# The last attention by groups of four heads, its gate turned through memory ahead of the product

## The reference

```python
def swa_sinks(q, k, v, sinks):                    # after rms_norm and rope of q and k
    ...                                            # n = 2 blocks of 128; kk, vv: the block before and the own one
    scores = jnp.einsum('bnihgd,bnjhd->bnhgij', qb, kk).astype(jnp.float32) * (d ** -0.5)
    ...                                            # band: at most 127 tokens back
    m = jnp.maximum(jnp.max(scores, axis=-1, keepdims=True), sink)
    p = jnp.exp(scores - m)
    p = p / (jnp.sum(p, axis=-1, keepdims=True) + jnp.exp(sink - m))
    o = jnp.einsum('bnhgij,bnjhd->bnihgd', p.astype(v.dtype), vv)

def odd_mixer(h, w_in, q_norm_w, k_norm_w, sinks, w_out, pos):
    ...
    o = swa_sinks(q, k, v, sinks).reshape(b, s, ATTN_WIDTH)
    return (o * jax.nn.silu(gate)) @ w_out
```

## Time and profile before

| | |
|---|---|
| median of 3 runs (lowest, highest) | 1905.14 us (1904.91, 1905.21) |
| span of the profiled execution, from first to last instruction | 1903.2 us |
| PE busy | 1896.5 us, 100% |
| DVE busy | 1269.8 us, 67% |
| ACT busy | 1001.4 us, 53% |
| DMA | 375.85 MB, 197 GB/s over the span |

### The profile page before, as it was taken

One profiled execution on the slowest core, in us unless ns is written; L12 is line 12 of the kernel. 1 busy time (PEld: TensorE's weight loads), 2 busy tenths in 40 slices (PEclk: granted clock), 3 DMA queues, 4 the chain that ended last, 5 costly groups with the idle time before them and its releaser, 6 DMA issues.

```text
span 1903.2 us, 22788 instructions
## 1 busy us (share of the span) xinstructions
PE 1896.5 (100%) x8663; PEld 1561.5 (82%) x8663; DVE 1269.8 (67%) x1925; ACT 1001.4 (53%) x1410; POOL 14.4 (1%) x32
## 2 busy tenths in 40 slices
PE   9999999999999999999999999999999999999999
PEld 7888887888888888888888888888888888787887
DVE  6676566776666466665466776755766677777875
ACT  6777554454444344443444455654555554665653
POOL 0001000000000000000000000000000000000000
PEclk9999999999999999999999999999999999999999
DMA  9667754686666666666666686665676687555555
GB/s 326 199 189 183 208 178 133 200 258 195 194 192 196 192 188 193 197 195 195 192 194 193 219 268 194 194 192 175 196 210 194 192 261 214 164 170 165 153 170 177
DMA packets 212364, 375.85 MB, mean 197 GB/s; under 512 B 14672, under 2 KB 35968, under 8 KB 212256
## 3 DMA queue, kind: packets, MB, share of 16 engines
q1 hardware_dynamic: 211008, 371.65, 63.9%
q0 software_dynamic: 816, 2.11, 0.9%
q10 hardware_dynamic: 432, 0.66, 0.1%
HBM read 361.76 MB, written 12.60 MB: 197 GB/s over the span
## 4 chain that ended last, share of the span: by engine, by line
PE 98%; DVE 1%; ACT 0%; issue 0%; DVEq 0%; ACTq 0%
PE g L1151 31%; PE g L1153 31%; PE g L1152 31%; PE m L1220 1%; PE ob L1238 0%; PE ob L1237 0%; PE ob L1236 0%; PE m L1085 0%; DVE wl L1587 0%; PE m L1212 0%; PE m L1210 0%; PE m L1304 0%; PE ob L1291 0%; DVE st L1596 0%; PE ob L1285 0%; PE m L1093 0%
## 5 line engine op out<-in xcount | busy, mean ns | idle before, releaser
L1587 DVE TENSOR_TENSOR wl<-raw,wh 128x1024 fp32r<-128x1024 f32 (+1 forms) x660 | 802.6, 1217 | 555.3 <-ACT wh L1334 551.9
L1334 ACT ACTIVATE wh<-raw 128x1024 fp32r<-128x1024 f32 (+1 forms) x661 | 695.5, 1053 | 746.1 <-PE g L1153 739.4
L1151 PE MATMUL g<-wh,xh 128*128 128x512 f32 x1886 | 741.0, 393 | 0.0
L1153 PE MATMUL g<-wh,xl 128*128 128x512 f32 x1886 | 734.6, 389 | 0.0
L1152 PE MATMUL g<-wl,xh 128*128 128x512 f32 x1886 | 734.0, 389 | 0.0
L1151 PEld LDWEIGHTS g<-wh,xh 128*128 128x128 f32 x1886 | 354.1, 188 | 77.7 <-issue 4.8
L1153 PEld LDWEIGHTS g<-wh,xl 128*128 128x128 f32 x1886 | 354.0, 188 | 74.3
L1152 PEld LDWEIGHTS g<-wl,xh 128*128 128x128 f32 x1886 | 354.2, 188 | 72.1
L1151 PE MATMUL g<-wh,mh 128*128 128x512 f32 x732 | 287.3, 392 | 0.0
L1153 PE MATMUL g<-wh,ml 128*128 128x512 f32 x732 | 285.0, 389 | 0.0
L1152 PE MATMUL g<-wl,mh 128*128 128x512 f32 x732 | 284.9, 389 | 0.0
(11 more groups left out here) (150 smaller groups left out, 818.5 us busy)
## 6 DMA issues: line engine op xcount, KB each, us to landing
raw<-in_ev_w_in SPq DMA_DIRECT2D x128, 512.0 KB, 3.8
raw<-in_w_in SPq DMA_DIRECT2D x92, 512.0 KB, 4.3
raw<-in_w_gate SPq DMA_DIRECT2D x88, 512.0 KB, 4.4
raw<-in_w_up SPq DMA_DIRECT2D x88, 512.0 KB, 4.3
raw<-in_w_down SPq DMA_DIRECT2D x88, 512.0 KB, 4.7
raw<-in_od_w_in SPq DMA_DIRECT2D x72, 512.0 KB, 4.2
raw<-in_w_out SPq DMA_DIRECT2D x32, 512.0 KB, 4.8
raw<-in_ev_w_out SPq DMA_DIRECT2D x32, 512.0 KB, 4.9
```

Of the source, the lines that this page charges most:

```text
L1151: e.matmul(o, hi[:, kt, c], h, start=first, stop=False)
L1153: last = e.matmul(o, lo[:, kt, c], h, start=False, stop=end)
L1334: return e.activation(o, i, AF.Copy, scale=scale)
L1587: return e.tensor_tensor(o, a, b, op)
```

## The change

The heads go in groups of four, g = 0 to 7. `oqk` makes the scores of four heads in one visit (three banks `m` and `ob`), `omax` the maxima of four heads in two reductions, `oexp` the exponentials of one head, and one of the four sinks with the last. `oapt` are three visits of four transposes. `oapv` has V stationary and the turned probabilities moving, two heads side by side on the two halves of PE's columns, so that `ob` receives the values turned: columns of a head on partitions, tokens along the row. ACT copies them to AW. Apart from that, `od_gate` puts the reciprocal of the sums onto the gate (`ogate`), and the gate, not the product, goes through memory (`turn`, `send`, `fetch`). `msent` then multiplies on DVE, rounds on ACT and subtracts on DVE. A `msent` of M5 is said no sooner than its `oapv`, and the lane of the heads starts after q is turned and no more after the gate's block.

```diff
@@ Plan
             for k in range(2):
                 yield 3 if k else 1
                 say("oq_turn", a[0], k)
+            self.lanes["att"].append(self.od_heads(a[0]))
...
             say("og", a[0], b.i)
-            yield 1
-            self.lanes["att"].append(self.od_heads(a[0]))
...
         yield 6 if p[0] == "xsent" else 4
+        while p[:2] == ("msent", "M5") and ("oapv", p[4]) not in self.said:
+            yield 1
         self.say(*p)
...
+        for g in (2 * j, 2 * j + 1):
+            say("oqk", g)
+            yield 1
+            yield from self.made("oqk", g)
+            say("omax", g)
+            yield 2
+            yield from self.made("omax", g)
+            for i in range(4):
+                say("oexp", g, i)
+                yield 1
+                if i == 2:
+                    say("oapt", g, 0)
+            self.spawn(self.od_gate(g))
+            yield from self.made("oexp", g, 3)
+            for i in (1, 2):
+                say("oapt", g, i)
+                yield 1
+            yield from self.made("oapt", g, 2)
+            say("oapv", g)
+            yield 2
+
+    def od_gate(self, g):
+        while not any(p[:2] == ("og", g // 2) for p in self.said):
             yield 1
+        yield from self.made("oexp", g, 3)
+        self.say("ogate", g)
+        yield 1
+        yield from self.turned_and_sent("msent", "M5", 2 * g, "o", g)
@@ PE
+                elif kind == "oqk":
...
+                    for i in range(3):
+                        on.wait_ge(*bank_free("oqk", g, i))
+                    on.wait_ge(ob_by[ob_free[p][0]], ob_free[p][1])
+                    for i in (0, 2):
+                        heads = [(od_bank(g, n), qo[rows_of(n), j % 2, 2 * (g % 2) + n // 2, :],
+                                  ko[rows_of(n), j, :]) for n in (i, i + 1)]
                         for o, q, k in heads:
                             e.matmul(o[:, 0:128], q[:, 0:128], k[:, 0:128], start=True, stop=True)
+                        for n, (o, q, k) in enumerate(heads):
                             e.matmul(o[:, 128:384], q[:, 128:256], k[:, 0:256], start=True,
+                                     stop=True).then_inc(s_pv if i + n == 3 else s_bank, 1)
...
+                elif kind == "oapv":
...
+                    v = vo[:, :, 64 * (g // 2):64 * (g // 2) + 64]
+                    for i in (0, 2):
+                        for n in (i, i + 1):
+                            e.matmul(OB[rows_of(n), 128 * i:128 * i + 256], v[:, 0, :], od_turned(n)[0],
+                                     start=True, stop=False, skip_group_check=True)
+                        for n in (i, i + 1):
+                            last = e.matmul(OB[rows_of(n), 128 * i + 128:128 * i + 256], v[:, 1, :], od_turned(n)[1],
+                                            start=False, stop=True, skip_group_check=True)
@@ ACT
+                    if a[0] == "M5":
+                        on.wait_ge(s_oprod, a[3] + 1)
+                        copy(hi[:, kt:kt + 2, :], AW[:, 0:512].rearrange("p (c t) -> p c t", c=2)).then_inc(s_split, 1)
+                        continue
...
+                elif kind == "oexp":
...
+                    for kb, (lo, hi) in enumerate(((0, 128), (128, 384))):
+                        last = e.activation(PB[:, i, lo:hi], PB[:, i, lo:hi], AF.Exp, bias=mx[:, h, kb:kb + 1],
+                                            accum_out=sm[:, h, kb:kb + 1])
+                    if i == 3:
+                        last = act(es[:, hs, :], es[:, hs, :], AF.Exp)
@@ DVE
                     on.wait_ge(*back(p))
+                    if a[0] == "M5":
+                        on.wait_ge(s_ob_act, ob_n[("oapv", a[3])])
+                        for c in range(2):
+                            o = tokens(AW[:, 256 * c:256 * c + 256])
+                            last = tt(o, o, read_back(p, c), ALU.mult)
+                        last.then_inc(s_oprod, 1)
+                        on.wait_ge(s_split, splits[p])
+                        tt(lo[:, kt:kt + 2, :], AW[:, 0:512].rearrange("p (c t) -> p c t", c=2),
+                           hi[:, kt:kt + 2, :].bitcast(f32), ALU.subtract).then_inc(s_sent, 1)
+                        continue
...
+                elif kind == "ogate":
...
+                    on.wait_ge(*steps.mark(tt(sm[:, hs, :], sm[:, hs, :], es[:, hs, :], ALU.add)))
+                    on.wait_ge(*steps.mark(e.reciprocal(ri[:, hs, :], sm[:, hs, :])))
...
+                    tt(AW[:, 512:1024].rearrange("p (t h d) -> p t h d", t=2, h=4),
+                       so[:, j % 2, :, c:c + 256].rearrange("p t (h d) -> p t h d", d=64),
+                       ri[:, hs, :].rearrange("p h t -> p t h").unsqueeze(3).to_broadcast([128, 2, 4, 64]),
+                       ALU.mult).then_inc(s_gated, 1)
```

More of the change, by code:

```diff
@@ L1061, in aw_free @@
             before = [q for q in plan.order[:plan.order.index(p)]
-                      if q[0] == "mix" and q[3] == "o" or q[:2] == ("turn", "msent")]
-            if not before:
-                return s_bank, 0
-            return full(*before[-1]) if before[-1][0] == "mix" else (s_turn, sents[before[-1][1:]])
+                      if q[:2] == ("turn", "msent")]
+            return (s_turn, sents[before[-1][1:]]) if before else (s_bank, 0)
         def weights(e, u):
@@ L1821, in vector @@
-                    last.then_inc(s_max, 1)
+                    reduce(mx[:, h:h + 1, 1:2], L[:, 128:384].unsqueeze(1), ALU.max, True).then_inc(s_max, 1)
+                elif kind == "oqk":
+                    g = a[0]
+                    if g:
+                        on.wait_ge(*full("oapt", g - 1, 2))
+                    else:
+                        on.wait_ge(s_sent, sents[last_sent("msent", "M4", 6)])
+                        on.wait_ge(*full("apt", "d", 7))
+                    for i in range(4):
+                        if i < 3:
+                            on.wait_ge(*full(*p, i))
+                        else:
+                            on.wait_ge(s_pv, opened[p])
+                        stt(PB[:, i, :], od_bank(g, i)[:, 0:384], 64 ** -0.5, C("band"), ALU.mult,
+                            ALU.add).then_inc(s_bank_dve if i < 3 else s_ob_dve, 1)
+                elif kind == "omax":
+                    g = a[0]
+                    hs = slice(4 * g, 4 * g + 4)
+                    on.wait_ge(*moved("oqk", g, 2))
+                    on.wait_ge(s_ob_dve, ob_n[("oqk", g)])
+                    reduce(mx[:, hs, 0:1], PB[:, :, 0:128], ALU.max, True)
+                    on.wait_ge(*steps.mark(reduce(mx[:, hs, 1:2], PB[:, :, 128:384], ALU.max, True)))
+                    on.wait_ge(*steps.mark(tt(mx[:, hs, :], mx[:, hs, :],
+                                              nsink[:, hs].unsqueeze(2).to_broadcast([128, 4, 2]), ALU.min)))
+                    tt(es[:, hs, :], mx[:, hs, :], C("sink", 4 * g, 4 * g + 4).unsqueeze(2).to_broadcast([128, 4, 2]),
+                       ALU.add).then_inc(s_omax, 1)
```

183 lines of the change are left out of this document (81 added, 102 removed).

## The result

| | before | after |
|---|---|---|
| runs, us | 1905.03 (1904.86 to 1905.21, 4 runs) | 1912.14 (1911.53 to 1912.50, 4 runs) |
| span of the profiled run, us | 1903.2 | 1909.7 |
| TensorE (PE) busy, us | 1896.5 | 1889.2 |

The changed kernel is slower: the ratio is 1.0037, with a 95% interval of 1.0025 to 1.0049. Forecast were 1910.1 us and a range of 1901 to 1916. The medians differ by 7.1 us. The profiled run was the quickest of the four; its span grew by 6.5 us, where the sum of the prediction had 5.0.

The account below looks back on a forecast made before the run. TensorE (PE), 98% of the span, was taken as the bound. -11.0 - 2.7 + 6 + 10.1 + 2.6 = +5.0 on the 1903.2 span gave 1908.2; with 1.9 for the median, 1910.1 us, range 1901 to 1916.

Parts of the forecast that it names:

- content of the visits: PE's attention visits (scores, transposes, values): 37.4 us for 48.4 before, so -11.0 (-12.5 to -0.6).
- old waits go: PE's waits in the attention, 1640 to 1903 us, in the kernel before: 2.7 us, which go.
- new waits in the attention: PE waits ahead of groups' transposes and one main unit, on longer ACT and DVE links: +6 (0 to 10).
- the tail: Behind the last value visit PE stands for the last gate fetch, queued behind SP's weight loads: +10.1 (9.3 to 10.9).
- the clock: Behind the tail's stand PE works at half clock for up to some 6 us: +2.6 (0 to 3.1).
- The term of the halves of the columns: In value visits two heads run beside each other on PE's column halves; taking turns would add 1.3 us a visit.
- The content alone: Rival: the fetch is back in time and new waits are no more than the old: 1894 us, chance 0.10.
- A tail with kind waits and no fallen clock: Rival: the tail stands, attention waits 2.7 or less, clock stays up or falls late: 1903 us, chance 0.25.
- ACT and DVE as the bound: Rival: in each group links come a cut later, waits of 10, main matmuls late: 1914 us, chance 0.10.
- The halves taking turns: Rival: column halves take turns in the value visits, +10.4, 1920 us, chance 0.05.

Follow-up runs that it names:

- the best version: Changed kernel with the last output product's third part for three column blocks, the last fetch ahead of the loads, its rows taken one weight half earlier: 1899.76 us.

## Why the prediction was right, and where its sizes were off

Term by term, on the profiled execution:

| step of the prediction | forecast | measured | |
|---|---|---|---|
| content of the visits | -11.0 | -10.7 | 8 x 1.72 + 24 x 0.44 + 8 x 1.67 = 37.7 for 48.4 |
| old waits go | -2.7 | -2.8 | 1.25 at 1711.67, 1.12 at 1728.81, 0.4 elsewhere |
| new waits in the attention | +6 | +8.4 | below |
| the tail | +10.1 | +9.55 | 9.77 less a pitch |
| the clock | +2.6 | +1.8 | nine slow matmuls |
| sum | +5.0 | +6.25 | the spans differ by 1909.7 - 1903.2 = 6.5 |

The signs of the terms, their places and their causes came as forecast. That the sum did too is partly luck: the waits were 2.4 us too small and the tail and the clock together 1.35 too large. Another 0.5 us of the miss in the median (1912.14 for 1910.1) is the profiled run, quicker than the median by more than before.

**The content** came as worked out, both from one visit each. The term of the halves of the columns rested on one row of another stage; with the halves made to take turns a visit cost 1.29 more. The Trainium skill's rule (TensorEngine Tiling (Array Packing), "When to Use Tiling": swap a narrow moving side and tile by columns, up to 2x) holds here: 1.8 by the visit, less by the fixed coming and going.

**The old waits** came right from a row that doesn't show them: the 1.6 us of the earlier trace rows are of weight loads (PEld), not of matmuls, and a wait of 0.8 on `m L1085` is missing there. From start to start PE did lose 2.8 us.

**The waits in the attention** are the mis-sized term, by 2.4 us. By group, against the prediction: group 0 1.2 (1.0), group 1 1.2 and 0.1 (1.4 and 0.4), group 2 1.0 (0.9), group 3 1.2 (0.8), group 5 0.5 (0.3), group 6 0.2 (0.6), groups 4 and 7 none (none), the unit that needs tiles 12 and 13 1.1 (1.1). These sum to 6.4, close to the 6 taken and the 6.5 worked out; single groups are off by up to 0.4 either way. Three that the prediction has not make the rest: 0.7 ahead of group 0's second transposes, and 0.6 and 0.7 ahead of main matmuls behind those of 1719.95 and 1775.96, for a weight half on DVE. The first of these:

```profile
1720.75 0.50 PE L1167 MATMUL g<-wh,xh 128*128 128x512 f32 x1 [0.41 <-DVE wl L1642]
```

The step looked for the wait at each group's exponentials and not at the weight halves queued with them. The runs showed that the two hang together: asked for later, the waits went over to the weight halves (6.8 for 1.3 us), and with 0.4 us taken off ACT five of those at the transposes fell by 0.37 each. That both are one backlog is the likeliest reading, not shown. What would empty it wasn't found; the table load of 1.28 us ahead of the exponentials is a large piece that does no work, and taking it away wasn't tried.

**The tail** was right in place, cause and size. The fetch left 3.3 us behind PE's last start (forecast 2.8 and the load's issue of 0.37), it took 4.1 for 4.8, the rest 2.4 for 2.3. One thing the prediction had as fixed wasn't: with the fetch ahead of the loads it landed in about 2.6 us.

**The clock** fell as forecast, and the term was too large by 0.8: it took PE's slow time at the start, up to 6 us, for the slow time behind the stand, which was 3.7 us. The record has the half clock from 1870.6 us, 6.5 us of it while PE still stood. What sets its length isn't shown. Filling the gap gave 1.7 to 2.3 us. The Trainium skill's rule (TensorE: Matmul & The Clock Gate, "Why this matters for your kernels": gaps between bursts bring the half rate back) is borne out by the stand of 9.55 us, and in some runs by one of 2.0. What the prediction had not seen is that a shorter stand needn't cost less: 5.2 us of standing left 13 slow matmuls where 9.55 had left nine.

**The rivals.** The content alone didn't decide as the kernel stood; in the best version it does, with the attention's waits taken off it: 1899.76 against 1905.0. A tail with kind waits and no fallen clock (1903) falls: the waits are 8.4 and the clock halved. ACT and DVE as the bound stands in part (8.4 us, about 1 a group, for the 10 it asked). The halves taking turns fell at 1921.5.

The balance of the best version closes too: PE's last matmul starts 11.8 us earlier than in the changed kernel, for 9.55 + 1.8 + 1.1 (tiles 12 and 13) - 0.8 (group 7's transposes) = 11.65.

## What to carry to other kernels

When a change puts a trip through memory on the last link ahead of a product, count the work that PE has between the link's start and its first reader, and then every in-order queue it passes: here SP's loads cost 4.4 us and the transfer without them 2.6, and once the loads were out of the way DVE's order was what PE waited for. The edit that gave most was neither a faster link nor an earlier one but a product that asks for those rows later (10.5 us of 12.4, though its outputs cost 1.25 of what PE gained). And a wait on an engine that is behind moved when it was postponed, and shrank when that engine's list was shortened.

## What the runs showed of the hardware that I had not expected

- A stand of 5.2 us of PE was followed by more slow matmuls (13) than one of 9.55 us (9), and one of 2.0 us by some too in the two profiled runs that had it (0.38 to 0.43 us apart); waits of 1.2 us in the attention were not, the granted clock stayed at 1.00 there.
- A fetch of 256 KB landed in 2.6 to 2.7 us in three kernels with no load issued just ahead of it (the gated rows' sends apart), and in 4.1 us in two that issued it half a microsecond behind a load of 512 KB.
- ACT's reading of its accumulator lasts 0.19 us in the record but holds up the next instruction by 0.10.
- With eight outputs issued within 8 us the last one landed 3.4 us behind its issue, and 2.2 us where they were spread out.
